# x as SyncE's first load, the last four modulation slabs on VectorE beside the gates, and head rows, group sums and router weights at other places in their queues

## The reference

```python
mod = silu(c) @ w_ada + b_ada                       # 6144 values
sh1, sc1, g1, sh2, sc2, g2 = split(mod, 6)          # shift, scale, gate, twice
n1 = rmsnorm(x, norm1_g) * (1 + sc1) + sh1
glu_in, z, xbc, dt_raw, gate_in = split(n1 @ w_in)
u = silu(layernorm(causal_conv31(u_a * sigmoid(u_b))))     # from glu_in
y = state_space(silu(causal_conv4(xbc)), softplus(dt_raw)) * silu(z)
y_ssm = rmsnorm_in_4_groups(y) @ w_ssm_out
h = x + g1 * ((g_cv * (u @ w_cv_out) + g_ssm * y_ssm) @ w_mix_out)
n2 = rmsnorm(h, norm2_g) * (1 + sc2) + sh2
h = h + g2 * experts(n2)       # router: n2 @ w_grp, n2 @ w_er
```

## Time and profile before

| | us |
|---|---|
| median of 3 runs | 3426.86 (3425.78 to 3430.24) |
| the profiled execution, its time | 3427.49 |
| its span, first to last instruction | 3425.9 |
| PE busy in the span | 2783.0 (81%) |
| VectorE busy | 934.7 (27%) |
| PE busy in 0 to 66 us | 25.11 |
| PE busy in 253 to 291 us | 17.89 |
| PE busy in 600 to 650 us | 32.19 |
| mean granted TensorE clock | 0.919 |

### The profile page before, as it was taken

One profiled execution on the slowest core, in us unless ns is written; L12 is line 12 of the kernel. 1 busy time (PEld: TensorE's weight loads), 2 busy tenths in 40 slices (PEclk: granted clock), 3 DMA queues, 4 the chain that ended last, 5 costly groups with the idle time before them and its releaser, 6 DMA issues.

```text
span 3425.9 us, 37786 instructions
## 1 busy us (share of the span) xinstructions
PE 2783.0 (81%) x13865; PEld 1349.5 (39%) x13866; DVE 934.7 (27%) x1758; ACT 699.3 (20%) x1218; POOL 242.9 (7%) x353
## 2 busy tenths in 40 slices
PE   5995899799965666666666656998899999989999
PEld 2443443344442222222222222455654435465444
DVE  2566599202131000000000003511530125026201
ACT  2216102002021111111111101214531012064210
POOL 1004102001000000000000010000120000003100
PEclk8998999899977888888888887999999999998999
DMA  7238221221216999999999982321002023200020
GB/s 202 100 134 301 106 74 49 74 74 67 81 64 240 424 424 424 425 424 424 425 424 424 425 334 103 105 81 49 1 26 74 25 100 112 74 25 1 32 88 28
DMA packets 126912, 605.22 MB, mean 177 GB/s; under 512 B 16372, under 2 KB 27220, under 8 KB 101220
## 3 DMA queue, kind: packets, MB, share of 16 engines
q1 hardware_dynamic: 108768, 579.03, 42.4%
q0 software_dynamic: 12128, 17.52, 2.0%
q10 hardware_dynamic: 5924, 7.41, 0.6%
HBM read 588.73 MB, written 15.11 MB: 176 GB/s over the span
## 4 chain that ended last, share of the span: by engine, by line
PE 60%; DMA 24%; DVE 10%; ACT 3%; issue 2%; POOL 1%; SPq 0%; ACTq 0%; DVEq 0%; POOLq 0%
PE PS L1600 54%; DMA S<-in_w 20%; PE PS L753 4%; DVE S L2230 3%; PE PS L954 1%; DVE RSTD L1267 1%; DMA S<-in_x 1%; DMA ring<-decay_rows 1%; DVE TAIL L1287 1%; DVE RSTD L2054 1%; DMA S<-sorted_rows 1%; ACT TAIL L1152 0%; ACT TAIL L1150 0%; ACT TAIL L1148 0%; DVE S L2058 0%
## 5 line engine op out<-in xcount | busy, mean ns | idle before, releaser
L1600 PE MATMUL PS<-nT,ring 128*128 128x512 f32 x2432 | 1068.9, 599 | 27.2 <-DVE nT L2058 10.3
L1600 PEld LDWEIGHTS PS<-nT,ring 128*128 128x128 f32 x2432 | 465.6, 193 | 609.8 <-issue 596.8
L1600 PE MATMUL PS<-ring,S 128*32 128x256 f32 (+2 forms) x3448 | 349.7, 547 | 179.0 <-DMA ring<-in_w 136.2
L1600 PE MATMUL PS<-S 128*32 128x256 f32 (+3 forms) x3328 | 358.5, 548 | 139.6 <-DMA S<-in_w 118.4
L1600 PE MATMUL PS<-S,ring 128*128 128x512 f32 x896 | 386.2, 592 | 2.5 <-DVE S L1418 1.7
L1600 PEld LDWEIGHTS PS<-ring,S 128*32 128x32 f32 (+1 forms) x3448 | 148.4, 130 | 351.2 <-issue 318.2
L1600 PEld LDWEIGHTS PS<-S 128*32 128x32 f32 (+1 forms) x3328 | 136.3, 133 | 312.6 <-issue 266.2
L1600 PEld LDWEIGHTS PS<-S,ring 128*128 128x128 f32 x896 | 170.0, 190 | 216.6 <-issue 216.6
L595 DVE TENSOR_TENSOR S<-S,PS 128x128 f32<-128x128 f32 x65 | 18.7, 288 | 720.9 <-ACT S L512 720.9
L2230 DVE SCALAR_TENSOR_TENSOR S<-S,COL 128x512 f32<-128x512 f32 x240 | 169.0, 779 | 0.1
L512 ACT ACTIVATE S<-PS 128x128 f32<-128x128 f32 x65 | 18.0, 278 | 544.3 <-PE PS L1600 544.3
(11 more groups left out here) (351 smaller groups left out, 2206.3 us busy)
## 6 DMA issues: line engine op xcount, KB each, us to landing
ring<-in_w SPq DMA_DIRECT2D x96, 2048.0 KB, 21.6
S<-in_w SPq DMA_DIRECT2D x96, 2048.0 KB, 21.6
ring<-in_w_in SPq DMA_DIRECT2D x40, 2048.0 KB, 7.9
ring<-in_w_ada SPq DMA_DIRECT2D x12, 2048.0 KB, 8.1
TAIL<-decay_rows SPq DMA_DIRECT2D x20, 640.0 KB, 5.4
expert_rows<-S POOLq DMA_DIRECT2D x65, 128.0 KB, 10.4
ring<-in_w_ssm_out SPq DMA_DIRECT2D x4, 2048.0 KB, 7.9
ring<-in_cmp_w SPq DMA_DIRECT2D x4, 2048.0 KB, 8.3
```

Source lines behind the costliest of these rows:

```text
L1600: return pe.matmul(o, l, r, start=start, stop=stop)
```

## The change

x becomes the first load of SyncE's queue, ahead of the slabs; PE transposes three of its chunks before the vectors, three after them and two after the first rows. The reciprocal for the first norm goes ahead of the wait for the modulation columns. Modulation slabs 8 to 11 leave their place behind the xbc products: they stand in the list behind a gate slab or an ssm slab, all four are taken by VectorE (16 products before the first `MIX`, 16 before the fifth) into `ADAL`, and PE turns their columns (`last_columns`) behind the mean. `MOD[:, 16:32]` is made where `MOD[:, 16:48]` was; the rest is made behind the centring. VectorE's scalar for the products is a column of `COL` (a second SiLU in place). Head rows 0 and 1 are loaded ahead of the last xbc slab, rows 2 and up ahead of the third GLU slab as before; the first GLU slab is now slab 14 of the list and not 18. VectorE masks the first group before the differences of head 2. Group sums on PE come one z chunk later, the last between the second and third gate chunk; the group norms on VectorE come one z step later; GpSimd adds up group 3 before the last channel pair; the first ssm half waits for 8 of the 16 normed chunks only. SyncE loads the router weights ahead of the first mix slab.

The diff, cut to its core:

```diff
-        ADA_AFTER = {7: (4,), 11: (5,), 15: (6,), 19: (7,), 23: (8, 9, 10, 11)}
-        ADA_VECTOR = range(4, 9)
+        ADA_AFTER = {7: (4,), 11: (5,), 15: (6,), 19: (7,)}
+        ADA_VECTOR, ADA_LATE = range(4, 12), 8
...
         for cb in range(2):
+            GATE_AT[cb] = len(slabs)
             slabs.append((cols(w_in, W_GATE + D + 512 * cb), "gate_product", 4 * cb + 4))
+            ada_slab(ADA_LATE + 2 * cb)
             for kh in range(2):
+                SSM_AT[cb, kh] = len(slabs)
                 slabs.append((cols(a["w_ssm_out"][0], 512 * cb, r0=1024 * kh), "ssm_product", 8 * cb + 4 * kh + 4))
+            ada_slab(ADA_LATE + 2 * cb + 1)
...
+            sp.dma_start(X0, a["x"][0].rearrange("(t p) d -> p t d", p=P)).then_inc(S("x_landed"), 16)
...
-                if i == GL0 + 1:
+                if i == XBC_AT[KX // 4 - 1]:
                     decay_rows(range(2))
...
+                if i == MX0:
+                    sp.wait_ge(S("ssm_product"), 16)
+                    sp.dma_start(WR[:, :, 0:NGRP], cols(a["w_grp"][0], 0, NGRP)).then_inc(S("router_landed"), 16)
+                    sp.dma_start(WR[:, :, NGRP:72], cols(a["w_er"][0], 0, NEXP)).then_inc(S("router_landed"), 16)
...
+            group_squares(3)
             channel_pair(6)
-            group_squares(3)
...
+            def last_columns():
+                pe.wait_ge(S("ada_step"), KD * len(ADA_VECTOR))
+                for n in range(12 - ADA_LATE):
+                    for i in range(4):
+                        m = mm(PS[:, 6, 4 * n + i:4 * n + i + 1], ADAL[:, n, P * i:P * i + P], ones[:, 0:1], True, True)
+                m.then_inc(S("ada_cols"), 12 - ADA_LATE)
...
-            later_columns(8)
-            for n in (9, 10, 11):
-                ada_row(n, 3 + n % 2)
...
-                if c % 4 == 1 and c > 4:
+                if c % 4 == 2 and c > 4:
...
                     for j in range(4):
                         if cb:
                             pe.wait_ge(S("gate_sig"), j + 1)
+                        elif j == 2:
+                            pe.wait_ge(S("rstd_root"), 1 + 2)
+                            group_sum(3)
+                        elif j == 3:
+                            pe.wait_ge(S("rstd_root"), 1 + 3)
...
-                        pe.wait_ge(S("norm_scaled"), AFTER["yn_ready"] + KI)
+                        pe.wait_ge(S("rstd_root"), 1 + 4)
+                        pe.wait_ge(S("norm_scaled"), AFTER["yn_ready"] + 8 * kh + 8)
...
             mm(PS[:, 4, :], ones[:, :], VSUM, True, True).then_inc(S("mean_mm"), 1)
+            last_columns()
...
-                    if c % 4 == 0:
+                    if c >= 6 and c % 4 == 2:
                         root(3 + (c // 4 - 1) % 2, 512, c // 4, "zsum")
+            root(4, 512, 4, "zsum")
...
-            for h in range(AHEAD):
+            for h in range(AHEAD - 1):
                 differences(h)
             group_masked(0)
+            differences(AHEAD - 1)
             group_masked(1)
...
-                if c >= 6 and c % 4 == 2:
-                    g = (c - 6) // 4
+                if c >= 7 and c % 4 == 3:
+                    g = (c - 7) // 4
                     rstd()
...
+            for step in range(32, 48):
+                ada_product(step)
             for n in range(KD):
+                if n == 4:
+                    for step in range(48, 64):
+                        ada_product(step)
...
+            dve.wait_ge(S("ada_cols"), 12)
+            link(dve.tensor_tensor(MOD[:, 32:48], PS[:, 6, 0:16], COL[:, C_BADA + 32:C_BADA + 48], ALU.add))
+            gain(32, C_N2)
```

More of the change, by code:

```diff
@@ L1610, in stats, with x_turn @@
                     stat[0] += 1
+            def x_turn(k):
+                if k >= 3:
+                    pe.wait_ge(S("xT_ready"), k - 2)
+                for t in range(NT):
+                    m = pe.transpose(PS[:, 1 + k % 3, P * t:P * t + P], X0[:, t, P * k:P * k + P], ident[:, :])
+                m.then_inc(S("transposed"), 1)
             pe.wait_ge(S("const_ready"), 11)
+            pe.wait_ge(S("x_landed"), 16)
+            for k in range(X_FIRST):
+                x_turn(k)
             pe.wait_ge(S("vec_landed"), 16 * N_VEC)
@@ L1618, in _ @@
             pe.transpose(PS[:, 7, 128:192], VEC[0:64, 5, :], ident[0:64, 0:64]).then_inc(S("transposed"), 1)
+            for k in range(X_FIRST, X_SECOND):
+                x_turn(k)
             pe.wait_ge(S("scalar_milestone"), AFTER["silu_c_ready"] + 1)
[L1621 to L1629, removed]
             def later_columns(n):
@@ L1654, in _ @@
             first_rows(0)
-            pe.wait_ge(S("x_landed"), 16)
-            for k in range(KD):
-                if k >= 3:
-                    pe.wait_ge(S("xT_ready"), k - 2)
-                for t in range(NT):
-                    m = pe.transpose(PS[:, 1 + k % 3, P * t:P * t + P], X0[:, t, P * k:P * k + P], ident[:, :])
-                m.then_inc(S("transposed"), 1)
+            for k in range(X_SECOND, KD):
+                x_turn(k)
             stats(4, KD)
@@ L1822, in _ @@
                 if n % 4 == 0:
-                    s = SO0 + 3 * cb
-                    landed(pe, s)
-                    w = v3(slot(s), 512)
+                    landed(pe, GATE_AT[cb])
+                    w = v3(slot(GATE_AT[cb]), 512)
                     for j in range(4):
@@ L1832, in _ @@
                     for kh in range(2):
-                        landed(pe, s + 1 + kh)
-                        w = v3(slot(s + 1 + kh), 512)
-                        pe.wait_ge(S("norm_scaled"), AFTER["yn_ready"] + KI)
+                        landed(pe, SSM_AT[cb, kh])
+                        w = v3(slot(SSM_AT[cb, kh]), 512)
+                        pe.wait_ge(S("rstd_root"), 1 + 4)
+                        pe.wait_ge(S("norm_scaled"), AFTER["yn_ready"] + 8 * kh + 8)
                         pe.wait_ge(S("u_ready"), KD)
@@ L1915, in root @@
                 roots[0] += 1
-            act.wait_ge(S("transposed"), AFTER["vec_turned"] + 6)
+            act.wait_ge(S("transposed"), X_FIRST + 6)
             act.activation(COL[:, :], PS[:, 0, :], ACT.Copy).then_inc(S("scalar_milestone"), 1)
@@ L1941, in _ @@
             for c in range(KX + 1):
-                if c == KX:
-                    for n in (9, 10, 11):
-                        ada_copy(n)
                 if c == 1:
@@ L2080, in _ @@
             gain(8, C_N1)
-            rstd()
             for k in range(KD):
@@ L2232, in _ @@
                             .then_inc(S("tap") if k < CONV_K - 1 else S("v_ready"), 1)
-            for c in range(z_at, KI + 3):
+            for c in range(z_at, KI + 4):
                 z_step(c)
             dve.wait_ge(S("m_ready"), HEADS)
+            dve.wait_ge(S("v_ready"), KD)
+            for step in range(32, 48):
+                ada_product(step)
             for n in range(KD):
+                if n == 4:
+                    for step in range(48, 64):
+                        ada_product(step)
                 dve.wait_ge(S("gate_sig"), n + 1)
```

66 lines of the change are left out of this document (21 added, 45 removed).

## The result

The changed kernel takes 3373.18 us, median of four runs (3369.37 to 3381.43), against 3426.32 of the kernel before beside it (3423.86 to 3430.24): a ratio of 0.9847 with a 95% interval of 0.9828 to 0.9866, 53.1 us less. Measured again, in five rounds beside two more kernels, it was 3373.0 (3366.34 to 3378.44) and 0.9837 (0.9823 to 0.9851). The forecast was 3373, faster.

A forecast was written before the change was run, and what follows sets the result against it. PE's waits in the first 1010 of 3426 us were taken as the bound, with later work started by the router's result. 8.7 + 23.8 + 19.6 - 3.8 + 6.1 = 54.4 off 3427.5 gave 3373, range 3359 to 3391.

The forecast's parts named there:

- part 2: Gap before the heads: modulation slabs 8 to 11 moved out and head rows earlier start the first pair 23.8 us sooner.
- part 3: z chunks, group sums and gates: gates start at 599 instead of 619.9; gain 19.6 us.
- part 1: Start: x first and the reciprocal ahead of the columns bring first scaling to 55.4 instead of 64.1; gain 8.7 us.
- part 4: Last modulation columns behind the mean: 32 small PE matmuls that nothing absorbs; loss 3.8 us.
- Rival A: Start: vectors land early and slab 1 uses the time before the first hole; 3 us more, 3370; chance 0.12.
- rival B: New wait: first half, ring rows slow (3379); second half, fourth group's sum or norm late (3380); both 3386; chance 0.22.
- (a): z stage on VectorE: group 2's norm goes behind z step 15, which comes at 603 instead of 609.66.
- (b): z stage on GpSimd: group 3 goes ahead of the last channel pair, done at about 606.5.
- (c): z stage on PE: later group sums remove 1.2 and 5.8 us waits; gate's first two chunks need only z chunks read.
- rival D: Ring slots freed late by VectorE stall PE, if slab 9's products end 43 us later: 34 over, 3461; chance 0.02.
- Part 5: Router: weights loaded at about 800 by SyncE end its products at 990.1 instead of 996.3; gain 6.1 us.
- Rival C: Start gains nothing because the slabs move later too; 3382; chance 0.04.

The follow-up runs named there:

- fifth kernel: Changed kernel with GpSimd's six scattered loads of DSK and HG issued late, behind the first modulation columns: 3354.23 us, first scaling at 39.33.
- fourth kernel: Changed kernel without SyncE's wait for the small vectors ahead of the second modulation slab: 3388.13 us, first scaling at 68.56.
- eighth kernel: Changed kernel with the six scattered loads late and without SyncE's wait for the vectors: 3368.02 us, first scaling at 51.71.
- third kernel: Changed kernel with head rows 0 and 1, GpSimd's group 3 order and the router weights' load put back: 3381.75 us.
- second and third kernel: The second is the changed kernel with VectorE's group norms one z step earlier again: 3376.56 us; third kernel has its own line.
- seventh kernel: Changed kernel with the whole old order of the z and gate stage put back, modulation slabs left as changed: 3401.72 us.
- sixth kernel: Changed kernel with the 32 late column matmuls behind PE's fourth convolution-gate chunk, ahead of its wait for GpSimd: 3370.19 us.
- second of the last three: Changed kernel with scattered loads late, columns at the variance and SyncE's vector wait ahead of the first modulation slab: 3353.76 us, ratio 0.9778.
- x back: Changed kernel with x loaded by ScalarE behind the vectors again and PE's transposes behind the first rows: 3374.29 us.

## Why the forecast held, point by point

**The sum.** 54.4 us were forecast and the medians differ by 53.1. Part of the closeness is luck: part 2 was 2.4 us too good and part 3 1.0 too low, and part 1 and part 4 hit in the profiled execution by errors that cancel, while other executions of the same code lie 1.5 to 3 us off in each.

**Part 1: size near, road wrong.** The first scaling came at 54.94, forecast 55.4; but in five more executions with this start it came at 56.4 to 58.0, so the forecast was about 2 us too good. Of its steps, x at 8.5 (measured 9.1) and the fourth slab near 50 (50.6) held. The vectors at 14 failed: 24.9, since they had not all landed when the first hole began. Without the hole they need until 17.0 (fifth kernel), so it caught them by about a microsecond. At 15 to 16 us GpSimd's queue held the engines, in the queues of the kernel after:

```profile
q0 software_dynamic: 15, 0.00, 783.2%
q10 hardware_dynamic: 93, 0.05, 16.7%
```

The second slab was issued behind them at 24.9, stood until about 33, and then three slabs ran in one piece, 17 us. That this ends where the forecast's two holes with bytes between them ended is part luck. The last row sum took 1.92 us here, not 3.64, with PE idle for only 1.5 us before it; this and the slab's extra 1 us nearly cancel. In the five other executions it took 2.4 to 3.6, which is a part of why they came later. What the forecast didn't see is that the holes were the larger prize: they were in its rows, taken as given.

**Rival A** falls with the 24.9 and with the fourth and the eighth kernel. The turn by packets of the Trainium skill (DMA: Bandwidth & Descriptors, Queues, rings and completion order), by which small vectors would be served beside a slab, does not forecast these landings if the profile's packets are those of the page, which no run here shows: 56 packets against 15, and 46.1 us where the slabs were not held back.

**Part 2: right in kind, 2.4 us too good.** The term that was mis-sized is the group products: sized 4.62 us from the earlier trace rows, they took 7.27. In the kernel before, PE came to them from modulation rows; now it comes from 4.4 us of idleness. The window of 248 to 256 us shows the granted clock:

```profile
248.00:256.00 8.00, 7.27 (x28) 5.84 (x28) 1.80 (x6) 7.90 (x17) 6.68 (x10) 0.64 0.95 372
```

0.64 as a mean, so that most of these 8 us ran at the lower of the clock's two levels, 1.2 GHz. In the eleven kernels of the experiments the group products took 6.3 to 7.3 us. The 2.65 us more are the whole miss (the wait behind them was 0.3 shorter than forecast). The rest is as told: the three rows for the ring slot did not come late, so rival B's first half did not happen. The early place of rows 0 and 1 did nothing (third kernel). The slabs and VectorE's order of masking were not put back; that the gain is theirs is read from the waits that went, not shown by a run.

**Part 3: right, 20.65 against 19.6.** The 1.05 us are z products that ended 0.9 sooner, a wait 0.5 shorter, and gates and sum 0.35 longer than forecast. The z products ended at 557.1 and the gates started at 565.6: 8.5 us for ScalarE's 16th SiLU, where the forecast had 9. The ordered group-3 sum cost nothing; rival B's second half did not happen either. Of its three moves, (a) and (b), which the forecast counted as needed, carry nothing alone (second and third kernel): the two gate chunks ahead of the sum, 14 us at full clock, cover either. That (c) carries the gain by itself is argued from these and the seventh kernel, not shown.

**Covered slabs and rival D.** ssm to mean took 144.20 us in every kernel with the slabs there, 144.19 before. Slab 9's products ended at 616.3, measured from the first ssm product 19.5 us behind it; the forecast had 22. Slabs 10 and 11 followed at 63 and 96 us, forecast 62 and 98. Rival D's point, 43 us later, was never near.

**Part 4: 3.91 against 3.8, in part by luck.** The columns are 3.73; two terms that the forecast lacked, 1.67 us of slower matmuls behind them and 1.3 given back in the next stretch, nearly cancel here. In other profiles they do not: against 57.95 before, the same order cost 2.2 us once and 5.6 twice. "Nothing absorbs it" holds for that place; 20 us further down the wait of 3.95 us takes them whole (sixth kernel).

**Part 5: 5.73 against 6.1.** The wait for the weights is gone; PE starts with ScalarE's first bias, and its 64 matmuls take 15.49 us from there instead of 13.93, the first 16 at the pace of the biases. Timeline of PE after:

```profile
926.28 15.49 PE L1607 MATMUL PS<-S,nT 128*128 128x72 f32 x64 [5.89 <-ACT nT L2030]
```

**Rival C** fails: the start gained 9.2, and some 7 in the other executions. Of the three signs that the forecast named for being wrong, no ring slab was waited for between 630 and 800 and the first pair came 16 us behind the products; but the tail did differ from 2429.6, at 2426. It varies by 10 us between kernels whose tail is the same, so this sign could not tell right from wrong.

## What to carry to other kernels

Find out what makes a hole in the DMA rates before ordering loads around it: here moving six tiny scattered loads out of the start was worth 17 us, more than giving the 2 MB input first place (3 to 6). Small loads that the next step needs want the large ones held for them: without that the start lost 11 to 14 us, whereas holding the first slab or only the second made no difference that can be told. When an engine's order has a short wait further down, put small independent work into that wait and not in front of full-clock matmuls, and put each moved piece of a group back alone: three of those tried here carried nothing by themselves.

## What the runs showed of the hardware

Six loads of 4-byte elements (4.0, 0.5 and 1.5 KB, two of each) stop the traffic of all queues of the core twice for 5 to 8 us, in both places where they were tried; the 15 packets of 15 to 16 us above took 8.4 us each (783.2% of 16 engines' microsecond).

And the small vectors, issued before 7 us, land according to what else is on the way:

| on the way beside the vectors | landed, us |
|---|---|
| x alone (second of the last three) | 11.3 |
| one slab, x behind them (kernel before, x back) | 11.6, 12.4 |
| x and one slab (fifth kernel) | 17.0 |
| x and one slab, and the holes (changed kernel) | 24.9 |
| x and three slabs (eighth kernel) | 28.2 |
| x and three slabs, and the holes (fourth kernel) | 46.1 |
